# Moving the first low-part subtractions of an expert loop from VectorE to GpSimd

## The reference, cut to what matters

```python
def moe(xn, w_router, b_router, w_gate, b_gate, w_up, b_up, w_down, b_down):
    logits = (xt @ w_router + b_router).astype(jnp.float32)
    top_vals, top_idx = lax.top_k(logits, TOP_K)          # 4 of 32 experts for each token
    gates = jax.nn.softmax(top_vals, axis=-1)
    ...                                                   # tokens sorted by expert, in blocks
    def expert_block(args):
        xb, e = args
        gt = jnp.minimum(xb @ w_gate[e] + b_gate[e], SWIGLU_LIMIT)
        up = jnp.clip(xb @ w_up[e] + b_up[e], -SWIGLU_LIMIT, SWIGLU_LIMIT)
        hdn = (up + 1.0) * (gt * jax.nn.sigmoid(SWIGLU_ALPHA * gt))
        return hdn @ w_down[e] + b_down[e]
    ...
    return out                                            # each token's four rows, weighted and summed
```

## Time and profile before

| | |
|---|---|
| median of 3 runs | 1580.83 us (1580.54 to 1581.74) |
| profiled execution, its own time | 1580.54 us |
| its span, first to last instruction | 1578.8 us |
| PE busy | 1430.6 us, 91% of the span |
| DVE busy | 1294.9 us, 82% |
| ACT busy | 951.5 us, 60% |
| POOL busy | 267.4 us, 17% |
| mean granted TensorE clock | 0.95 |

### The profile page before, as it was taken

How to read it: one execution, slowest core, us unless ns; L and a number is a source line. 1 busy time by engine, 2 the same in 40 slices (tenths; PEclk the granted TensorE clock), 3 DMA queues, 4 the chain that set the end, 5 groups by cost and what they waited for, 6 DMA issues and landing times.

```text
span 1578.8 us, 19232 instructions
## 1 busy us (share of the span) xinstructions
PE 1430.6 (91%) x6488; PEld 1091.9 (69%) x6488; DVE 1294.9 (82%) x950; ACT 951.5 (60%) x708; POOL 267.4 (17%) x282
## 2 busy tenths in 40 slices
PE   3996189966999999999999999999999999999981
PEld 2885047764777777777777777777777777777761
DVE  5899553358888888888888888888888888888885
ACT  3230153234677777777777777777777777777751
POOL 2387750012100000000000000000000000000043
PEclk9998569966999999999999999999999999999996
DMA  7900310066999999999999999999999999999955
GB/s 228 341 16 27 126 73 1 1 217 252 346 375 374 375 376 372 376 370 378 371 372 364 372 367 381 373 375 373 378 369 370 377 365 369 369 377 374 374 180 195
DMA packets 84048, 476.44 MB, mean 302 GB/s; under 512 B 10715, under 2 KB 11014, under 8 KB 34870
## 3 DMA queue, kind: packets, MB, share of 16 engines
q1 hardware_dynamic: 71518, 432.48, 71.7%
q0 software_dynamic: 6560, 23.55, 4.5%
q10 hardware_dynamic: 5944, 20.08, 3.4%
HBM read 448.44 MB, written 27.63 MB: 302 GB/s over the span
## 4 chain that ended last, share of the span: by engine, by line
PE 83%; POOL 6%; issue 4%; DMA 3%; DVE 2%; ACT 1%; SPq 1%; POOLq 0%; ACTq 0%
PE pair L1583 22%; PE pair L1582 22%; PE pair L1581 22%; PE pair L1588 3%; POOL area_t L559 3%; PE pair L1405 2%; PE pair L1406 2%; PE pair L1407 2%; PE pair L1561 2%; PE pair L1568 2%; DMA h<-in_x 1%; PE pair L1447 1%; PE pair L1466 1%; POOL ring L559 1%; PE pair L1456 1%
## 5 line engine op out<-in xcount | busy, mean ns | idle before, releaser
L1153 DVE TENSOR_TENSOR w_low<-w_raw,w_high 128x2048 fp32r<-128x2048 f32 x380 | 865.0, 2291 | 127.3 <-ACT w_high L812 127.2
L812 ACT CAST w_high<-w_raw 128x2048 fp32r<-128x2048 f32 x380 | 726.6, 1913 | 312.0 <-PE pair L1583 312.0
L1583 PE MATMUL pair<-w_high,xT_low 128*112 128x512 f32 x1024 | 404.6, 395 | 0.0
L1581 PE MATMUL pair<-w_high,xT_high 128*112 128x512 f32 x1024 | 404.4, 395 | 0.0
L1582 PE MATMUL pair<-w_low,xT_high 128*112 128x512 f32 x1024 | 404.2, 395 | 0.0
L1582 PEld LDWEIGHTS pair<-w_low,xT_high 128*112 128x112 f32 x1024 | 179.4, 175 | 57.4
L1581 PEld LDWEIGHTS pair<-w_high,xT_high 128*112 128x112 f32 x1024 | 179.6, 175 | 56.6
L1583 PEld LDWEIGHTS pair<-w_high,xT_low 128*112 128x112 f32 x1024 | 179.4, 175 | 56.3
L1581 PE MATMUL pair<-w_high,hT_high 128*112 128x512 f32 x512 | 201.9, 394 | 0.0
L1583 PE MATMUL pair<-w_high,hT_low 128*112 128x512 f32 x512 | 201.9, 394 | 0.0
L1582 PE MATMUL pair<-w_low,hT_high 128*112 128x512 f32 x512 | 201.0, 393 | 0.0
(11 more groups left out here) (259 smaller groups left out, 1420.0 us busy)
## 6 DMA issues: line engine op xcount, KB each, us to landing
w_raw<-in_w_gate SPq DMA_DIRECT2D x128, 1024.0 KB, 7.0
w_raw<-in_w_up SPq DMA_DIRECT2D x128, 1024.0 KB, 6.3
w_raw<-in_w_down SPq DMA_DIRECT2D x128, 1024.0 KB, 6.3
y_rows<-area_m ACTq DMA_DIRECT2D x32, 448.0 KB, 4.2
ring<-in_w_in SPq DMA_DIRECT2D x5, 2048.0 KB, 19.0
y_rows<-area_t SPq DMA_DIRECT2D x1, 8064.0 KB, 37.7
ring<-in_w_out SPq DMA_DIRECT2D x2, 2048.0 KB, 10.5
h<-in_x SPq DMA_DIRECT2D x4, 512.0 KB
```

The lines of the kernel that those rows point to most:

```text
L812: s.copy(w_high[:, i % HIGH_RING, :], w_raw[i][:, :]).then_inc(high_ready, 1)
L1153: v.tensor_tensor(w_low[i][:, :], w_raw[i][:, :], w_high[:, i % HIGH_RING, :].bitcast(F32), ALU.subtract).then_inc(low_ready, 1)
L1581: t.matmul(to[half], tok_high, hi, start=False, stop=False)
L1583: last = t.matmul(to[half], tok_low, hi, start=False, stop=(k == KD - 1))
```

## The change

GpSimd takes over four subtractions of VectorE: the low parts of the first three weight pieces and the low part of the gate's bias rows. They stand in GpSimd's stream ahead of its wait for the token table. GpSimd waits for its own bias subtraction before it goes on. On VectorE, the rest of the bias rows and `xT_low_part(0)` move behind the slot, overflow and gate arithmetic, with a wait for GpSimd's part of `bias_split`, and one for `low_ready` 3 ahead of `xT_low_part(0)`, so that `low_ready` is counted in order. TensorE waits for all three counts of `bias_split` ahead of `gate(0)` and no longer in `down`.

```diff
@@ gpsimd
+            for i in range(AHEAD):
+                pool.wait_ge(high_ready, i + 1)
+                g.tensor_tensor(w_low[i][:, :], w_raw[i][:, :], w_high[:, i, :].bitcast(F32), ALU.subtract).then_inc(low_ready, 1)
+            pool.wait_ge(bias_high, 3)
+            pool.wait_ge(low_ready, AHEAD)
+            g.tensor_tensor(bias_gu[32:64, :], bias_stage[32:64, :], bias_gu[32:64, :].bitcast(F32),
+                            ALU.subtract).then_inc(bias_split, 1)
+            pool.wait_ge(bias_split, 1)
             pool.wait_ge(table_ready, 1)
@@ vector
-            low_part(0, 0)
             dve.wait_ge(table_done, 1)
             v.tensor_copy(tok_tab[:, :], bank[1][0:CAP, 0:COLS]).then_inc(table_ready, 1)
-
-            dve.wait_ge(bias_high, 3)
-            v.tensor_tensor(bias_gu[32:64, :], bias_stage[32:64, :], bias_gu[32:64, :].bitcast(F32),
-                            ALU.subtract).then_inc(bias_split, 1)
-            v.scalar_tensor_tensor(bias_gu[96:128, :], bias_stage[96:128, :], 1.0, bias_gu[96:128, :].bitcast(F32),
-                                   ALU.add, ALU.subtract).then_inc(bias_split, 1)
-            low_part(1, 1)
...
-            xT_low_part(0)
-            low_part(2, 2)
...
+            dve.wait_ge(bias_high, 3)
+            dve.wait_ge(bias_split, 1)
+            v.scalar_tensor_tensor(bias_gu[96:128, :], bias_stage[96:128, :], 1.0, bias_gu[96:128, :].bitcast(F32),
+                                   ALU.add, ALU.subtract).then_inc(bias_split, 1)
             v.tensor_tensor(bias_d[32:64, :], down_stage[32:64, :], bias_d[32:64, :].bitcast(F32),
                             ALU.subtract).then_inc(bias_split, 1)
...
+            dve.wait_ge(low_ready, AHEAD)
+            xT_low_part(0)
             for i in range(DOWN):
                 at = i + AHEAD
                 low_part(at % DOWN, at)
@@ tensor
             def down(b, base, place=DOWN):
                 pe.wait_ge(sel_down_ready, b + 1)
-                if isinstance(b, int) and b == 0:
-                    pe.wait_ge(bias_split, 3)
...
             transpose_x(0)
-            pe.wait_ge(bias_split, 2)
+            pe.wait_ge(bias_split, 3)
             gate(0, 0)
```

More of the change, by code:

```diff
@@ L1251, in _, with turned, xT_low_part @@
             v.tensor_tensor(gates[:, :, :], gates[:, :, :], wide(gate_sum[:, :], TOP_K), ALU.mult).then_inc(gates_ready, 1)
+            dve.wait_ge(bias_high, 3)
+            dve.wait_ge(bias_split, 1)
+            v.scalar_tensor_tensor(bias_gu[96:128, :], bias_stage[96:128, :], 1.0, bias_gu[96:128, :].bitcast(F32),
+                                   ALU.add, ALU.subtract).then_inc(bias_split, 1)
             v.tensor_tensor(bias_d[32:64, :], down_stage[32:64, :], bias_d[32:64, :].bitcast(F32),
                             ALU.subtract).then_inc(bias_split, 1)
+            def turned():
+                return pair[3][:, :].rearrange("p (b t) -> p b t", b=2)[:, :, 0:4 * CAP]
+            def xT_low_part(b):
+                dve.wait_ge(xT_high_ready, b + 1)
+                v.tensor_tensor(xT_low[:, :, :], turned(), xT_high[:, :, :].bitcast(F32), ALU.subtract).then_inc(xT_low_ready, 1)
             def hT_low_part(b):
```

## The result

The changed kernel is slower: 1591.95 us (4 runs, 1590.1 to 1594.09) against 1581.28, a ratio of 1.0065 with a 95% interval of 1.0049 to 1.0081. The forecast was 1588.4 and at most 1591.5. The kernel got slower as forecast and by the mechanism that was forecast, but by 10.7 us and not by 7.6. The median lies 0.45 us above the range, as much as the kernel before came out above the 1580.83 on which the forecast stands. The medians of the three later measurements, 1589.57, 1590.59 and 1588.87, lie inside the range.

A forecast was written before the change was run, and what follows sets the result against it. TensorE was taken to bound the kernel, with `gate(0)` set by VectorE's routing and the gather. A hold of 8.9 less 1.3 gave +7.6 us: 1588.1 against the profiled execution, 1588.4 against the median; range 1584.5 to 1591.5.

The forecast's parts named there:

- Chain, and what VectorE gains: Around the first expert's start: removed VectorE subtractions are off the chain, gain 0; the 3.0 us stall ahead of `gate(1)` stays.
- GpSimd's price: GpSimd before the table: 4.5 us per piece subtraction, 2.3 for the bias piece, together 15.8 us.
- The hold: Routing chain: GpSimd and VectorE take turns by whole instructions with two SBUF operands, delaying VectorE by 8.9 us.
- The first partial rival: Routing chain: small VectorE instructions slip through, only those of 512 or more columns are held; net +4.2; held in part, 0.13.
- the second: Routing chain: by the page's rule only small copies within SBUF are held, comparisons pass; net +4.5; held in part, 0.13.
- win every turn: Routing chain: VectorE goes first, GpSimd's later pieces are put off until the chain is through; +9.4, 1590.2 us; chance 0.08.
- The gather: After the table: index copy and gather issue no longer held by VectorE's bias subtraction; -1.05 and -0.25, together -1.3 us.
- the bound of 0: At the gather: nothing comes back if VectorE's slot arithmetic or bias addition holds index copy and issue as before.
- 8.9 - 1.3 = +7.6 us ahead of `gate(0)`, kept to the end, since every later step is timed by TensorE.: From `gate(0)` to the end: the net +7.6 us delay passes on unchanged through the expert loop.

The follow-up runs named there:

- e10: Kernel before, with VectorE, once the table is written, waiting until GpSimd has issued the gather before its bias rows; ratio 1.0001.
- e3: Changed kernel with GpSimd's three piece subtractions behind the first gather's landing, the gate's bias subtraction on VectorE, first xT_low ahead of the low_ready wait; ratio 1.0048 to before.
- e1: Changed kernel with GpSimd's three piece subtractions cut from 2048 to 32 columns and the gate's bias subtraction back on VectorE; ratio 1.0017 to before.
- e4: Kernel before with nothing moved; GpSimd pauses 11.4 us between the table and the gather's index copy; ratio 1.0076.

## Why the prediction fell short, step by step

- **Chain, and what VectorE gains: right.** The removed subtractions gave nothing, and the 3.0 us ahead of `gate(1)` stayed.
- **GpSimd's price: right.** 4.5 us each and 2.34, against 4.5 and 2.3.
- **The hold: right as a mechanism and in its sum, +8.9 forecast, +8.6 measured; not right step by step.** Forecast were +1.6 at the comparison of 512 columns, +1.0 at that of 128 and +6.1 within the scan. Measured are +1.8 at the 16-column conversion, +4.2 at the comparison of 512, +0.8 at that of 128, +1.7 at the small copy, and nothing within the scan. The sum came out all the same, as the text said it would: it is GpSimd's work less what VectorE spends beside it. The first partial rival falls, as instructions of 16 and 32 columns are held in full; the second falls, as the two-input comparison is held. VectorE didn't win every turn.
- **The gather: a term mis-sized.** -1.3 forecast, -0.4 in the trace. VectorE's slot arithmetic has a two-input comparison of 0.74 us at 371.56, and the copy, issued with it, takes 0.78 us: I had named this as the bound of 0 and taken the other end. e10 shows that -1.2 was to be had, by VectorE standing still there. e3 shows how close it is: with the same order on VectorE the copy was issued 0.07 us ahead of that comparison, took 0.18, and gather was 8.81.
- **The step that failed: "8.9 - 1.3 = +7.6 us ahead of `gate(0)`, kept to the end, since every later step is timed by TensorE."** TensorE's steps themselves got longer: the clock came later and fell once more, +2.9 us in the trace of the first comparison, +1.8 as a mean of four traces each. The forecast had no term for TensorE's clock: I took the stages of one trace of before as fixed, and it is one of the three in four with the fewest slow matmuls. With it the sum is 8.6 - 0.4 + 2.9 = 11.1 us in the first pair of traces and 8.6 - 0.3 + 1.8 = 10.1 over four each, against the 7.6 forecast. The range should have had another 1 to 3 us upwards. That three of four medians fall into it is owed to its width, as no term of it is the clock's.
- **Left open:** why the changed kernel had the late clock in four traces of four and before in one of four. It isn't the hold alone, since e1 and e10 have 8 and 12 slow matmuls at the start with routing as short as before, and not the longer idling alone, since e4 is free of it. With so few traces, chance isn't excluded.

## What to carry to other kernels

GpSimd is no free helper for a chain of VectorE: here a long GpSimd instruction that reads SBUF held the next VectorE instruction with two SBUF inputs, and also conversions, copies and scalar operations within SBUF, until it ended, however small they were. Reductions and instructions with an input in PSUM went on. Before moving work there, lay its durations as blocks over the other's instructions. Put such work where VectorE reads PSUM or waits (no run here tries the same work in shorter pieces), and keep VectorE still for the moment in which GpSimd issues a gather that everything waits for. When TensorE restarts from idling, allow for its clock (1.8 to 2.9 us here) and take more than one trace.

## What was not expected of the hardware

A VectorE conversion of 16 columns took 1.95 to 2.08 us, 0.17 alone, while GpSimd subtracted. Behind a TensorE stall of the same 3.0 us the granted clock stayed in full in five traces and fell to half in the others for 5 to 12 matmuls (in e3_gather_first the stall was 3.4 us). And in every trace, of both kernels and of all the others, one GpSimd instruction of the mixer takes 33.1 us through VectorE's convolution (143.67 in the earlier trace rows, with the earlier trace rows), while in the routing chain GpSimd never waited longer than the rest of one VectorE instruction. No run shows what makes the difference.
